# First feed-forward of a two-block model: three entry units with high and low part side by side, the norm's factors earlier on VectorE, silu's table loaded earlier

## The reference, cut to what matters

```
h2 = rms_norm(x, norm_ffn_pre)                         # x: 256 x 1024
ff = (silu(h2 @ w_gate) * (h2 @ w_up)) @ w_down        # 1024 -> 2816 -> 1024
x  = x + rms_norm(ff, norm_ffn_post)
```

## Time and profile before

| | |
|---|---|
| device time, median of 3 runs | 805.73 us |
| lowest and highest | 805.39 and 805.81 us |
| span of the profiled execution | 804.3 us |
| VectorE, ScalarE, GpSimd busy | 71%, 58%, 14% |
| first feed-forward on TensorE | from about 279 us of the span to about 458 us |

### The profile page before, as it was taken

One profiled execution on the slowest core, in us unless ns is written; L12 is line 12 of the kernel. 1 busy time (PEld: TensorE's weight loads), 2 busy tenths in 40 slices (PEclk: granted clock), 3 DMA queues, 4 the chain that ended last, 5 costly groups with the idle time before them and its releaser, 6 DMA issues.

```text
span 804.3 us, 13652 instructions
## 1 busy us (share of the span) xinstructions
PE 798.1 (99%) x5838; PEld 700.9 (87%) x5838; DVE 570.7 (71%) x712; ACT 465.5 (58%) x614; POOL 108.7 (14%) x82
## 2 busy tenths in 40 slices
PE   9999999999999999999999999999999999999998
PEld 7999988788888898888888889987899888888886
DVE  5877996897576586766676688598978865556653
ACT  6679774665534575454454575477787644444442
POOL 0102790662000000000000010111610100000000
PEclk9999999999999999999999999999999999999999
DMA  9844444443653655554655555465323555555641
GB/s 312 296 168 158 159 158 158 152 165 113 214 169 146 222 189 172 206 187 180 210 174 192 208 167 203 165 211 167 129 90 109 202 179 187 209 173 194 202 165 52
DMA packets 37820, 143.03 MB, mean 178 GB/s; under 512 B 9426, under 2 KB 11490, under 8 KB 24320
## 3 DMA queue, kind: packets, MB, share of 16 engines
q1 hardware_dynamic: 36576, 138.69, 49.8%
q0 software_dynamic: 1040, 3.43, 1.2%
q10 hardware_dynamic: 144, 0.04, 0.0%
HBM read 141.08 MB, written 1.06 MB: 177 GB/s over the span
## 4 chain that ended last, share of the span: by engine, by line
PE 93%; DMA 3%; DVE 2%; ACT 1%; issue 0%; POOL 0%; SPq 0%; POOLq 0%
PE ps L2380 8%; PE ps L2373 7%; PE ps L2025 6%; PE ps L2274 6%; PE ps L2272 6%; PE ps L2273 6%; PE ps L1957 6%; PE ps L2031 6%; PE ps L2028 6%; PE ps L1958 6%; PE ps L1959 6%; PE ps L2378 4%; PE ps L2375 4%; PE ps L2133 2%; DMA raw<-w 1%; DMA x<-xT 1%
## 5 line engine op out<-in xcount | busy, mean ns | idle before, releaser
L1178 DVE TENSOR_TENSOR wlo<-raw,whi 128x2048 fp32r<-128x2048 f32 (+2 forms) x128 | 289.4, 2263 | 73.9 <-ACT whi L622 72.5
L622 ACT ACTIVATE whi<-raw 128x2048 fp32r<-128x2048 f32 (+2 forms) x128 | 241.3, 1887 | 105.7 <-DMA raw<-w 105.6
L1957 PE MATMUL ps<-xx,whi 128*128 128x256 f32 x396 | 114.2, 288 | 0.0
L1958 PE MATMUL ps<-xx,whi 128*128 128x256 f32 x396 | 112.0, 283 | 0.0
L1959 PE MATMUL ps<-xx,wlo 128*128 128x256 f32 x396 | 112.0, 283 | 0.0
L2272 PE MATMUL ps<-whi,xx 128*128 128x512 f32 x216 | 84.1, 389 | 0.0
L2273 PE MATMUL ps<-whi,xx 128*128 128x512 f32 x216 | 84.0, 389 | 0.0
L2274 PE MATMUL ps<-wlo,xx 128*128 128x512 f32 x216 | 84.0, 389 | 0.0
L2025 PE MATMUL ps<-whi,xx 128*128 128x512 f32 x208 | 83.0, 399 | 0.0
L2031 PE MATMUL ps<-wlo,xx 128*128 128x512 f32 x208 | 81.1, 390 | 0.0
L2028 PE MATMUL ps<-whi,xx 128*128 128x512 f32 x208 | 81.0, 390 | 0.0
(11 more groups left out here) (322 smaller groups left out, 1366.7 us busy)
## 6 DMA issues: line engine op xcount, KB each, us to landing
raw<-w SPq DMA_DIRECT2D x105, 1024.0 KB, 4.8
raw<-w SPq DMA_DIRECT2D x42, 512.0 KB, 4.8
raw<-w SPq DMA_DIRECT2D x8, 256.0 KB, 6.3
x<-xT SPq DMA_DIRECT2D x4, 256.0 KB, 5.7
work<-bias_scratch POOLq DMA_DIRECT2D x1, 1024.0 KB, 7.2
raw<-w SPq DMA_DIRECT2D x4, 192.0 KB, 3.2
out<-x SPq DMA_DIRECT2D x3, 256.0 KB, 2.5
raw<-w SPq DMA_DIRECT2D x3, 240.0 KB, 3.3
```

The source lines that it names most:

```text
L622: A(hi, full, ACT.Copy).then_inc(sem("hi_ready"), 1)
L1178: V.tensor_tensor(lo, full, hi.bitcast(F32), ALU.subtract)\
L1957: mm(out, hi, xh[:, tile, :], start=start, stop=False, skip_group_check=skip)
L1958: mm(out, hi, xl[:, tile, :], start=False, stop=False, skip_group_check=skip)
```

## The change

Units 44, 45 and 46 are computed the wide way too, so all gate and up units but 43 are wide. They get banks of their own (0 and 2; 3 and 4; 1 and 7). Unit 44 starts its high products when only the high part of its weights is there, as before, and waits for the low part ahead of the low products. The down products of pair 0, which use banks 3 to 6, wait in addition for `gate_r` 2, that is for the end of the scaling of gate 1.

ScalarE gets six more low copies: two of unit 44, ahead of and behind nothing but its own `split_hi` of units 46 and 47, and four of units 45 and 46. Those of unit 45 stand around `split_hi` of unit 48, behind `hidden_hi` of pair 0. A silu of one element stands ahead of `bc_copy` and brings silu's table load with it.

VectorE gets six more adds. The two of unit 44 stand behind `norm_factors` and ahead of `split_lo` of unit 46. `hidden_lo` of pair 0 moves behind the add, add and scale of gate 1. `split_lo` of unit 49 moves behind `hidden_lo` of pair 1, and the scale of silu (one on its own, `silu_scaled`) stands ahead of the up unit's adds.

The core of the diff:

```diff
-WIDE1 = range(2, PAIRS1)
+WIDE1 = range(1, PAIRS1)
+ENTRY_BANKS = ((0, 2), (3, 4), (1, 7))
...
-    units = []
+    units = [(U_F1 + 1, ENTRY_BANKS[0])]
...
             split_hi(U_F1 + RING)
+            low_copy(U_F1 + 1, 0, lows[1])
+            low_copy(U_F1 + 1, 1, lows[1])
             split_hi(U_F1 + 1 + RING)
+            A(warm[:, :], half_s[:, 0:1], ACT.Silu)
             bc_copy("n3")
             silu_pair(0)
             hidden_hi(0, "hid", 0, 0)
             for j in range(1, PAIRS1):
                 u = U_F1 + 3 * j - 1
-                wide = j in WIDE1
-                if wide:
-                    low_copy(u, 0, lows[0])
+                low_copy(u, 0, lows[0])
                 split_hi(u + RING)
-                if wide:
-                    low_copy(u, 1, lows[0])
-                    low_copy(u + 1, 0, lows[1])
+                low_copy(u, 1, lows[0])
+                low_copy(u + 1, 0, lows[1])
                 silu_pair(j)
...
             norm_factors("n3", 1)
+            up_added(U_F1 + 1, 0)
+            up_added(U_F1 + 1, 1)
             split_lo(U_F1 + RING)
             dve.wait_ge(sem("norm_bcs"), before("bcs", "n3") + 1)
-            gate_scaled(0, U_F1, U_F1 % RING)
+            gate_scaled(U_F1, U_F1 % RING)
             split_lo(U_F1 + 1 + RING)
-            hidden(0, 0, U_F1 + 1, (U_F1 + 1) % RING)
-            hidden_lo(0, 0, "hid", 0)
+            silu_scaled(0)
+            hidden_wide(0, 0)
             for j in range(1, PAIRS1):
                 u = U_F1 + 3 * j - 1
-                wide = j in WIDE1
-                if wide:
-                    gate_wide(j, u)
-                else:
-                    gate_scaled(j, u, u % RING)
+                gate_wide(j, u)
+                if j == 1:
+                    hidden_lo(0, 0, "hid", 0)
                 split_lo(u + RING)
-                if wide:
-                    up_wide(j, u + 1, 0)
-                if j < PAIRS1 - 1:
+                silu_scaled(j)
+                up_added(u + 1, 0)
+                if 1 < j < PAIRS1 - 1:
                     split_lo(u + 1 + RING)
-                if wide:
-                    up_wide(j, u + 1, 1)
-                    hidden_wide(j, j % 2)
-                else:
-                    hidden(j, j % 2, u + 1, (u + 1) % RING)
+                up_added(u + 1, 1)
+                hidden_wide(j, j % 2)
                 hidden_lo(j, j % 2, "hid", 0)
-                if j == PAIRS1 - 1:
+                if j in (1, PAIRS1 - 1):
                     split_lo(u + 1 + RING)
                 split_lo(u + 2 + RING)
...
             first_unit(U_F1, 8, "n3")
-            first_parts(U_F1 + 1, 8)
+            pe.wait_ge(sem("hi_ready"), U_F1 + 2)
+            used(wide_tiles(U_F1 + 1, 8, low=lambda: arrived(U_F1 + 1)))
             norm_stats("n3", sq3)
...
                 pe.wait_ge(sem("lo_ready"), u + 1)
-                if j in WIDE1:
+                if first:
+                    pe.wait_ge(sem("ple_copy"), PLE_EARLY // 2)
+                else:
                     pe.wait_ge(sem("gate_r"), j)
                     pe.wait_ge(sem("hid_y"), j)
-                    used(wide_tiles(u, 8))
-                else:
-                    used(pair_tiles(u, 8, between=lambda: norm_bc("n3")))
+                used(wide_tiles(u, 8, between=(lambda: norm_bc("n3")) if first else None))
                 pe.wait_ge(sem("lo_ready"), u + 2)
-                if j in WIDE1:
-                    used(wide_tiles(u + 1, 8))
-                else:
+                if first:
                     pe.wait_ge(sem("gate_r"), 1)
-                    used(pair_tiles(u + 1, 8))
+                used(wide_tiles(u + 1, 8, between=factors_read if first else None))
                 pe.wait_ge(sem("lo_ready"), u + 3)
                 pe.wait_ge(sem("hid_lo"), j)
                 if first:
-                    pe.wait_ge(sem("ple_copy"), PLE_EARLY // 2)
+                    pe.wait_ge(sem("gate_r"), 2)
```

More of the change, by code:

```diff
@@ L163, in wide_units @@
 def wide_units():
-    units = []
+    units = [(U_F1 + 1, ENTRY_BANKS[0])]
     for j in WIDE1:
-        units += [(U_F1 + 3 * j - 1, GATE_BANKS), (U_F1 + 3 * j, UP_BANKS)]
+        gate, up = ENTRY_BANKS[1:3] if j == 1 else (GATE_BANKS, UP_BANKS)
+        units += [(U_F1 + 3 * j - 1, gate), (U_F1 + 3 * j, up)]
     for j in WIDE2:
@@ L887, in _ @@
                     split_hi(u + 1 + RING)
-                if wide:
-                    low_copy(u + 1, 1, lows[1])
+                low_copy(u + 1, 1, lows[1])
                 hidden_hi(j, "hid", 2 * (j % 2), j % 2)
@@ L1504, in _, with gate_scaled @@
             ahead(U_PLE)
-            def gate_scaled(j, u, bank):
+            def gate_scaled(u, bank):
                 dve.wait_ge(sem("unit_used"), u + 1)
-                if not isinstance(j, int) or j >= 1:
-                    dve.wait_ge(sem("gated"), j)
                 V.tensor_tensor(two(silu), two(ps[bank][:, :]), factors_by_tile(2), ALU.mult).then_inc(sem("gate_r"), 1)
[L1514 to L1524, removed]
             def low_added(u, m, out, low):
@@ L1537, in gate_wide, with silu_scaled, up_added @@
                 V.tensor_tensor(two(silu), two(silu), factors_by_tile(2), ALU.mult).then_inc(sem("gate_r"), 1)
-            def up_wide(j, u, m):
-                if m == 0:
-                    dve.wait_ge(sem("silu"), j + 1)
+            def silu_scaled(j):
+                dve.wait_ge(sem("silu"), j + 1)
+                if j:
                     dve.wait_ge(sem("hid_y"), j)
-                    V.tensor_tensor(two(gated), two(silu), factors_by_tile(2), ALU.mult).then_inc(sem("gated"), 1)
+                V.tensor_tensor(two(gated), two(silu), factors_by_tile(2), ALU.mult).then_inc(sem("gated"), 1)
+            def up_added(u, m):
                 count(low_added(u, m, lows[1], lows[1]))
@@ L1550, in hidden_wide @@
                 dve.wait_ge(sem("dve_chain"), chained[0])
-                dve.wait_ge(sem("hid_lo"), j)
+                if j:
+                    dve.wait_ge(sem("hid_lo"), j)
                 V.tensor_tensor(hid[slot_h], two(gated), lows[1], ALU.mult).then_inc(sem("hid_y"), 1)
@@ L2351, in _, with wide_tiles @@
             used(ple_part(range(4, PLE_EARLY)))
[L2354 to L2363, removed]
+            def wide_tiles(u, base, between=None, low=None):
                 for m in range(2):
@@ L2373, in wide_tiles @@
                             mm(o[:, :], whi[:, u % SLOTS, w(k)], xx[:, base + k, :, :], start=k == 0, stop=False)
+                        if low:
+                            low()
                         for k in range(8):
@@ L2385, in _, with factors_read @@
             first_unit(U_F1, 8, "n3")
-            first_parts(U_F1 + 1, 8)
+            pe.wait_ge(sem("hi_ready"), U_F1 + 2)
+            used(wide_tiles(U_F1 + 1, 8, low=lambda: arrived(U_F1 + 1)))
             norm_stats("n3", sq3)
+            def factors_read():
+                pe.wait_ge(sem("norm_bcs"), before("bcs", "n3") + 1)
             def ffn1_step(j, u):
```

1 line of the change is left out of this document (removed).

## The result

The changed kernel takes 807.2 us (median of 12 runs, 806.38 to 808.2) against 805.61 us before in the same comparison. The ratio is 1.0020, with a 95% interval of 1.0013 to 1.0027, that is 1.0 to 2.2 us more. Forecast were 807.0 us, and 1.3 us more.

The account below looks back on a forecast made before the run. TensorE, busy 798.1 of 804.3 us, was taken to bound the kernel. The span of 804.3 plus 1.3 for the new wait for `hidden_lo` plus 1.4 around the span gave 807.0 us, range 805.0 to 808.2.

Parts of the forecast that it names:

- TensorE's own work: Unit 44 to the first down product: three wide units of 5.57 us, ready at 302.9, 0.6 to 0.8 us earlier.
- The factors: VectorE up to gate 0's scale: factors' copy at 292.64, two adds costing 0.68, scale 0.14 later, `bcs` 0.2 us ahead.
- The product of pair 0: On VectorE after gate 0's scale and silu: old order kept, so 0.14 us later, at 299.33.
- The chain behind it: ScalarE and VectorE from `hidden_hi` (300.05) through gate 1's copies, add and scale to `hidden_lo`; down products at 304.94, 1.3 us later.
- The hop to TensorE that no row had shown: From `hidden_lo`'s end on VectorE to the start of a waiting TensorE: taken as 0.1 us.
- The gap: TensorE's standstill ahead of the down products of pair 0, waiting for `hidden_lo`: about 2.0 us.
- What is late next: Pair 1 and gate 2: product of pair 1 at 308.4, 1.3 us to spare, no second gap.
- No new wait: Rival at the down products: only TensorE's saving stays, 805.0 us, or 805.2 with the smaller saving; chance 0.11.
- The factors come late: Rival at ScalarE's run ahead of `bc_copy`: a table load holding ScalarE 1.3 us more gives 808.1 us; chance 0.12.
- The clock falls in the gap: Rival: standstill drops TensorE to 1.2 GHz, down products take up to about 5 us more, 808 to 812 us; chance 0.05.

Follow-up runs that it names:

- e8_load_in_before: The kernel before with only a one-element silu added ahead of `bc_copy`, so the table load comes early; 806.28 us, ratio 1.0007 to the kernel before.
- e4_no_early_load: The changed kernel without the one-element silu, the table load back between `bc_copy` and silu of pair 0; 807.15 us, ratio 1.0018 to the kernel before.
- e9_half_split: The changed kernel with half of unit 48's high split written twice on ScalarE, ahead of gate 1's second low copy; 809.37 us, ratio 1.0046 to the kernel before.
- e5_second_split: The changed kernel with unit 48's whole high split written twice on ScalarE, ahead of gate 1's second low copy; 811.67 us, ratio 1.0069 to the kernel before.

## Why the prediction was right, step by step

The forecast was right, in size and in mechanism. Point by point, times of after less 0.23:
- *TensorE's own work.* Forecast: down products ready at 302.9, measured 303.34 - 0.23 = 303.11. The unit price of 5.57 was right for unit 46, but all of the 0.26 us around the sums and the factors' turning stayed and a little more came (0.33, 17.41 less 17.08); the saving is 0.50, outside the 0.6 to 0.8 of the forecast. The time didn't depend on it, since the chain below set the start of the down products.
- *The factors.* Forecast 292.64, measured 292.74. The two adds cost 0.66 (293.18 to 293.84), forecast 0.68. The scale of gate 0 is 0.22 later than before (forecast 0.14), and `bcs` was ready 0.33 us ahead of it (forecast 0.2).
- *The product of pair 0.* Forecast 299.33, measured 299.33: the 0.08 came back, because product follows scale by 0.72 instead of 0.80.
- *The chain behind it.* Forecast for `hidden_hi`, copy, split, copy, add, scale, `hidden_lo`, down: 300.05, 300.58, 300.86, 302.69, 303.08, 303.54, 304.15, 304.94. Measured: 300.06, 300.60, 300.86, 302.67, 303.07, 303.53, 304.14, 304.92. The hop to TensorE that no row had shown was 0.10, as taken.
- *The gap.* Forecast 2.0 us, measured 1.81. The difference is TensorE's own later end, which doesn't count in the time. What the sum left out is the slow first product behind the gap, 0.08 us. The rest of the way from the forecast 1.3 to the measured 1.6 is within the interval.
- *What is late next.* The product of pair 1 was forecast for 308.4 and came at 308.38, and TensorE had nothing to wait for at gate 2.
- *The rivals.* "No new wait" fell with the bracket of the first down product. "The factors come late" is a real mechanism, seen once (e8_load_in_before, 1.24 us of VectorE's waiting, set off by a late transfer and not by a longer load), but not in the changed kernel's profile; taking the load away changed nothing. From the load at 293.93 to the next instruction it is 1.30 us. "ScalarE: Activation LUTs" of the Trainium skill, section "What ACT_TABLE_LOAD costs", adds a drain of 1.38 us to the load; the trace shows none, here and in e4_no_early_load (294.94 to 296.23). "The clock falls in the gap" did not come in the changed kernel, but it was nearer than its chance of 0.05 said, as the mean clocks of e9_half_split suggest with 1.09 us more of gap and the profile of e5_second_split shows with 1.94 us more. My price for it, up to 5 us, was twice the 2.6 measured, because the clock was back before the down unit was over.

Shown by experiment is that the gap is owed to the order of the lists and not to the wide units: four other orders with the same units have no gap of more than 0.14 us, and are 1.7 to 1.9 us faster in the median (two of them in the same comparison as e4_no_early_load: 805.42 and 805.38 against 807.15). That a real saving of 0.50 us remains is shown by the traces (17.41 against 17.91, in three kernels). Four medians lie 0.3 to 0.5 us below before, but no single interval lies wholly below 1.0. Taken together, the means of these four kernels' executions lie 0.42 us below those of the kernel before, by my estimate from the times on record plus or minus 0.2, which is in line with the 0.50.

## What to carry to other kernels

When the busiest engine's work gets shorter by an operation that others have to finish (copy the right half, add it), price the new chain up to the next wait of the busiest engine, not the operations: here 0.50 us of saving met a chain that had lost 2.35 us of slack and ended 1.8 us after TensorE was ready. A short copy that someone waits for shouldn't stand behind a long one that nobody waits for yet, and an item whose reader is near shouldn't be moved behind items whose reader is far. Such a fault is removed by moving a line or two, so look at the wait's releaser before giving up the idea.

## What the runs showed of the hardware that I had not expected

- TensorE's granted clock stayed at 1.00 across a standstill of 1.65 us in the changed kernel and across one of 2.74 us in the profile of e9_half_split. In that of e5_second_split it fell to 0.50 when TensorE had stood still for 2.4 of 3.59 us, and was back after over 5 us of work. So one length of standstill doesn't decide it in these runs: with about 2.7 us the runs of one kernel fell in two groups, 3 and 3, 3.5 us apart. The level of 0.50 cost 2.6 us behind the gap of 3.59, so that this wait cost 6.2 us in all.
- Behind a standstill the first product of 512 columns takes 0.31 us to the next one instead of 0.23 (305.15 to 305.46 in the changed kernel's trace).
